# Scaling half of the gate one-hots on ScalarE instead of VectorE

## The chip, the cores and the metric

The kernel runs on one core of a Trainium2 chip. The metric is the device time of one execution in microseconds (us). Below, PE is TensorE, DVE is VectorE, ACT is ScalarE, POOL is GpSimd and SP is the engine that issues most of the transfers.

## The reference, cut to what matters

One encoder block over 512 tokens of width 1024: RMSNorm, a projection, a pooling mixer and forgetting attention, an output projection, and then PEER, a retrieval over 16384 experts. Only PEER is touched by the change:

```
top_s, top_pos = lax.top_k(cand_s, PEER_TOPK)            # 8 heads, 16 picks each, of 128 x 128 experts
gates = jax.nn.softmax(top_s, axis=-1)
a = gelu(einsum('thkd,td->thk', expert_u[idx], xb))
y = einsum('thk,thkd->td', gates * a, expert_v[idx])     # added to x
```

Everything is float32.

## The kernel before, in words

For the first 128 tokens (`FIRST`) the picked expert rows are gathered by indirect transfers and handled on DVE: one `dot` for each of the 128 picks (L1293) and one `add_row` for each (L1423). For the other 384 tokens (`DT`) the kernel works densely: it computes u . x for all 16384 experts in 128 chunks of 128 experts ("ups"), makes a dense gate matrix, multiplies the two and runs 128 chunks of a down product. Every matmul operand is split into a high and a low part (`three`, L746), so that an up chunk is 8 x 3 matmuls of 384 columns. The split of the weights is made by ACT (high part, `hi_to`, L514) and by POOL or DVE (low part).

The gate matrix of one token t is a 128 x 128 matrix: the sum over its 128 picks of gate * onehot(first index) * onehot(second index). That is one matmul of two one-hot matrices, contracted over the picks, one of them scaled by the gates. It is made in the gate stage, which lies under 48 of the up chunks (`UPS_GATE`). Tokens go in groups of four (`GROUP`), 96 groups (`GROUPS`) in all, two for each up chunk (`CHUNK_GROUPS`). `slotT` holds both indices turned so that picks lie on partitions; the turned gates stay in a PSUM bank (`GATE_BANK`).

For group g, with `oh` in two buffers (g % 2):

- DVE, L1403 to L1417: waits until PE has used group g - 2 (`oh_used`), compares (L1408, both one-hots of four tokens in one instruction), does one `dot` in eight of nine groups, waits for its own comparison (`fence`), and multiplies the first one-hot by the gates (L1415), which signals `oh_ready`.
- PE, L996 to L1006: inside an up chunk, ahead of its third and its seventh block of three matmuls (k = 2 and k = 6), waits for `oh_ready` and for a free PSUM bank (`gp_used`), and does the four matmuls of a group, which signal `oh_used`.
- ACT, L703 to L719: for each up chunk first copies both groups from PSUM to `gbuf` (L709, after `oh_used`), then does `up` (L677): the Gelu of the chunk (L683), the high split of the chunk four further on (L514), and each second time a store; then a store of a piece of the gates.

Ahead of the stage ACT copies the two turned index tiles (L698) and the counting row (L700), and does the `up` of the last chunk before the stage (L701). PE turns the gates (`turn(2)`, shown as L976) ahead of the last block of that chunk, and signals `tr_ready`. Each engine works through its instructions in this written order. The end of the up chunks is followed by `residual` (L1017) and by the quads of the down product (L1030), whose first operands come back from DRAM by SP (L386).

Of the kernel before, what the change touches and what calls it, by code (L numbers as in the profile page):

```python
# [8 lines left out]
ALU = mybir.AluOpType  # L9
ACT = mybir.ActivationFunctionType  # L10
AX = mybir.AxisListType

P = 128
# [26 lines left out]
RAW, SPLIT = 3, 4  # L40
# [3 lines left out]
DT = T - FIRST  # L44
# [3 lines left out]
GROUP = 4  # L48
GROUPS = DT // GROUP
# [13 lines left out]
UP_GATE = UP_SOFT + UPS_SOFT  # L63
UP_REST = UP_GATE + UPS_GATE
CHUNK_GROUPS = GROUPS // UPS_GATE
# [17 lines left out]
def program(nc, xvT, wst, consts, w_pool, keysT, uT, u, v, out):  # L83
# [6 lines left out]
    with ctx:  # L90
        def sb(name, shape, dt=F32, where=ctx, side=None):
            return where.enter_context(nc.sbuf_tensor(name, shape, dt, side=side))

        def sem(name):
            return ctx.enter_context(nc.semaphore(name))
# [65 lines left out]
        gates = ExitStack()  # L161
        oh = sb("oh", [P, 2, 2, GROUP, P], where=gates)
        sel = sb("sel", [P, 3, TB, PH, TOPK], where=gates)
        slotT = sb("slotT", [P, 2, DT], where=gates)
        junk = sb("junk", [P, D], BF16, gates)
        gates.close()
        gt.insert(0, sb("gt0", [P, SENT, QUAD * HALF], where=ups))
# [30 lines left out]
        bank = low + [wide[:, 0:T], wide[:, T:2 * T]]  # L198
# [4 lines left out]
        GATE_BANK, IOTA_BANK = 4, 5  # L203
# [34 lines left out]
        gd_ready, ge_ready, sel_ready = sem("gd_ready"), sem("ge_ready"), sem("sel_ready")  # L238
        tr_ready, tr_saved = sem("tr_ready"), sem("tr_saved")
        oh_ready, oh_used, gp_used = sem("oh_ready"), sem("oh_used"), sem("gp_used")  # L240
        gp_stored = [sem("gp_stored0"), sem("gp_stored1")]
        a_out = [sem("a_out0"), sem("a_out1")]
        picks_ready, rows_t_ready = sem("picks_ready"), sem("rows_t_ready")
# [86 lines left out]
        def a_of(j):  # L330

            return act_a[:, (j // 2) % 2, j % 2, :]

        def done_up(j):

            return j - UP_EARLY + NQ + 1
# [163 lines left out]
        def _(act):  # L500
            split = 0

            def hi_to(last):

                nonlocal split
                while split <= min(last, END_W - 1):
                    n, split = split, split + 1
                    if n in POOL_HI:
                        continue
                    act.wait_ge(*landed(n))  # L510
                    if n >= SPLIT:
                        act.wait_ge(w_used, n - SPLIT + 1)
                    part = slice(T, D) if n < 2 else slice(0, D)
                    act.activation(wh[:, n % SPLIT, part], raw_of(n)[:, part], ACT.Copy).then_inc(w_hi, 1)  # L514
# [162 lines left out]
            def up(j):  # L677

                n = UP_W + j - UP_EARLY
                if j % 2 == 0:  # L680
                    act.wait_ge(a_out[(j // 2) % 2], 16 * (j // 4))
                act.wait_ge(w_used, n + 1)
                act.activation(a_of(j), bank[n % 2][:, 0:DT], ACT.Gelu).then_inc(out_done, 1)  # L683
                hi_to(n + SPLIT)
                if j % 2:
                    act.wait_ge(out_done, done_up(j))
                    act.dma_start(a_dram[j // 2], act_a[:, (j // 2) % 2, :, :]).then_inc(a_out[(j // 2) % 2], 16)
# [11 lines left out]
            act.wait_ge(tr_saved, 2)  # L699
            act.activation(bank[IOTA_BANK][:, 0:P], iota, ACT.Copy).then_inc(tr_saved, 1)  # L700
            up(UP_GATE - 1)  # L701

            for j in range(UP_GATE, UP_REST):  # L703
                for g in range(CHUNK_GROUPS * (j - UP_GATE), CHUNK_GROUPS * (j - UP_GATE + 1)):
                    half, at = g // HALF_GROUPS, GROUP * (g % HALF_GROUPS)
                    if at == 0 and half >= 2:
                        act.wait_ge(gp_stored[half % 2], 16 * PIECES * (half // 2))
                    act.wait_ge(oh_used, g + 1)
                    act.activation(gbuf[:, half % 2, :, at:at + GROUP],  # L709
                                   bank[GP + g % 2][:, :].rearrange("j (t i) -> j i t", t=GROUP), ACT.Copy)\  # L710
                       .then_inc(gp_used, 1)
                up(j)
                full, piece = divmod(CHUNK_GROUPS * (j - UP_GATE + 1) // (HALF_GROUPS // PIECES), PIECES)
                if 1 <= full <= SENT:
                    half, rows = full - 1, slice(piece * NCH // PIECES, (piece + 1) * NCH // PIECES)
                    if piece == 0:
                        act.wait_ge(gp_used, FREE_BANKS + HALF_GROUPS * full)
                    act.dma_start(g_dram[half, :, rows, :], gbuf[:, half % 2, rows, :])\
                       .then_inc(gp_stored[half % 2], 16)  # L719
# [25 lines left out]
        def _(pe):  # L745
# [194 lines left out]
            for k in range(NQ):  # L940
# [7 lines left out]
                if k == 3:  # L948
                    pe.wait_ge(identr_ready, 1)
                    for kk in range(KD):  # L950
                        at = slice(kk * P, (kk + 1) * P)
# [6 lines left out]
            def up(n, static, between=None):  # L958

                pe.wait_ge(w_lo, n + 1)  # L960
                pe.wait_ge(out_done, n - (QUERY_W + 1))
                project(bank[static % 2][:, 0:DT], static % SPLIT, hh, hl, between, at=slice(FIRST, T))
# [31 lines left out]
            with pe.Fori(0, UPS_GATE // SPLIT) as it:  # L994
                for i in range(SPLIT):
                    def frames(k):  # L996
                        if k % 4 != 2:
                            return
                        of = CHUNK_GROUPS * i + k // 4
                        group = it * (CHUNK_GROUPS * SPLIT) + of  # L1000
                        pe.wait_ge(oh_ready, group + 1)
                        pe.wait_ge(gp_used, group + 1)
                        for t in range(GROUP):
                            last = pe.matmul(bank[GP + of % 2][:, t * P:(t + 1) * P], oh[:, of % 2, 1, t, :],  # L1004
                                             oh[:, of % 2, 0, t, :], start=True, stop=True)
                        last.then_inc(oh_used, 1)  # L1006

                    static = UP_W + UP_GATE - UP_EARLY + i
                    up(it * SPLIT + static, static, frames)
# [3 lines left out]
            def residual(b, done):  # L1013

                for half in range(2):
                    for kk in range(4):
                        last = pe.matmul(bank[done + half][:, kk * P:(kk + 1) * P], x[:, 4 * half + kk, b * P:(b + 1) * P],  # L1017
                                         ident, start=(kk == 0), stop=(b == 0 and kk == 3), is_transpose=True)
                return last

            pe.wait_ge(gp_used, FREE_BANKS + GROUPS)
            pe.wait_ge(oh_ready, GROUPS)
            residual(2, 2)
            residual(3, 4)
            pe.wait_ge(dots_done, PICKS)
# [32 lines left out]
        def _(dve):  # L1058
# [8 lines left out]
            def step(instruction):  # L1067

                nonlocal count
                count += 1  # L1070
                instruction.then_inc(dve_done, 1)

            def fence():

                dve.wait_ge(dve_done, count)
# [35 lines left out]
            for what, i in in_turn:  # L1111
# [45 lines left out]
                if what == "norm":  # L1157
                    n, c = i, i // 2
                    dst, g = (qn, QG) if i % 2 == 0 else (kn, KG)
# [64 lines left out]
                elif what == "mean":  # L1224
                    g, z = i, len(QK_W) + i
# [5 lines left out]
                    src, s = 0, 1  # L1231
                    while s < w:
# [4 lines left out]
                        src, s = dst, 2 * s  # L1237
# [15 lines left out]
                elif what == "score":  # L1253
# [16 lines left out]
                    for b in blocks:  # L1270
                        at, size = P if b == 1 else 0, (b + 1) * P
# [21 lines left out]
            def dot(j):  # L1293

                if j == 0:
                    dve.wait_ge(rows_t_ready, 1)
                dve.wait_ge(row_in[j % ROWS], 16 * (j // ROWS + 1))
                if j:
                    dve.wait_ge(dots_done, j)
                dve.scalar_tensor_tensor(junk[:, :], picked[:, j % ROWS, :], 1.0, wide[:, :], ALU.mult, ALU.mult,  # L1300
                                         accum_out=pick_a[:, j:j + 1]).then_inc(dots_done, 1)
# [101 lines left out]
            for g in range(GROUPS):  # L1403
                s, at = g % 2, slice(GROUP * g, GROUP * g + GROUP)
                if g >= 2:
                    dve.wait_ge(oh_used, g - 1)
                both = [P, 2, GROUP, P]
                step(dve.tensor_tensor(oh[:, s], bank[IOTA_BANK][:, 0:P].unsqueeze(1).unsqueeze(1).broadcast_to(both),  # L1408
                                       slotT[:, 0:2, at].unsqueeze(3).broadcast_to(both), ALU.is_equal))
                if g % 9 != 8 and g < GROUPS - 1:  # L1410
                    dot(DOTS_GATE + g - g // 9)
                fence()
                if g == 0:
                    dve.wait_ge(tr_ready, 3)
                dve.tensor_tensor(oh[:, s, 0], oh[:, s, 0],  # L1415
                                  bank[GATE_BANK][:, at].unsqueeze(2).broadcast_to([P, GROUP, P]), ALU.mult)\
                   .then_inc(oh_ready, 1)  # L1417
# [130 lines left out]
```

## Time and profile before

| | |
|---|---|
| time, median of 3 runs | 1440.97 us (1440.34 to 1442.09) |
| profiled execution | 1441.41 us |
| its span | 1439.4 us |
| PE busy | 1431.6 us (99%) |
| DVE busy | 1133.4 us (79%) |
| ACT busy | 574.4 us (40%) |
| POOL busy | 979.8 us (68%) |
| gate stage | about 596 to 883 us of the span |

A busy share is the time in which an engine executes instructions, as a share of the span; PE can be near 100% in stages in which it waits for nobody and in which only its own work counts. The order in which engines wait for one another stands in the waits and in the timeline.

### The profile page before, as it was taken

How to read it: one execution, taken by the hardware profiler on the slowest of the kernel's cores; microseconds unless marked ns; L12 is line 12 of the kernel's file. 1: busy time of each engine (PE TensorE's matmuls, PEld its weight loads, DVE VectorE, ACT ScalarE, POOL GpSimd, SP SyncE). 2: the span in 40 equal slices, each digit the busy share in tenths (PEclk: the TensorE clock that was granted, in tenths of full speed). 3: DMA queues.
4: the chain of work that ended last, by engine and by line, in shares of the span. 5: the costliest groups of instructions: out<-in, count | busy, mean ns of one | idle time of the engine just before them, and what ended most of it. 6: DMA issues, size and time to landing. Idle time of an engine off the chain costs nothing.

```text
span 1439.4 us, 20447 instructions
## 1 busy us (share of the span) xinstructions
PE 1431.6 (99%) x7551; PEld 1277.2 (89%) x7551; DVE 1133.4 (79%) x1876; ACT 574.4 (40%) x799; POOL 979.8 (68%) x533
## 2 busy tenths in 40 slices
PE   9999999999999999999999999999999999999998
PEld 7766798899999999999999999888888888888887
DVE  6678551769999999699999995498777777777775
ACT  5775453333333333444444444333333333333332
POOL 3421544346888788866766675599887888878883
PEclk9999999999999999999999999999999999999999
DMA  6221332235778888989999986998888888888883
GB/s 227 103 89 45 103 113 100 89 100 184 251 262 268 273 272 273 348 281 364 355 360 355 372 296 230 371 383 340 346 346 346 327 326 345 344 341 328 331 302 117
DMA packets 122293, 381.57 MB, mean 265 GB/s; under 512 B 11768, under 2 KB 28280, under 8 KB 122240
## 3 DMA queue, kind: packets, MB, share of 16 engines
q1 hardware_dynamic: 70384, 202.69, 39.5%
q0 software_dynamic: 36864, 134.23, 25.3%
q10 hardware_dynamic: 14992, 44.06, 7.8%
q8 instruction: 18, 0.29, 0.1%
q14 instruction: 35, 0.29, 0.1%
HBM read 336.89 MB, written 44.06 MB: 265 GB/s over the span
## 4 chain that ended last, share of the span: by engine, by line
PE 95%; DVE 2%; DMA 1%; ACT 1%; issue 0%; SPq 0%; DVEq 0%
PE bank L748 28%; PE bank L749 28%; PE bank L750 28%; PE bank L1004 6%; PE bank L936 1%; DMA wf<-a_dram 1%; PE bank L884 1%; PE bank L907 0%; PE wide L896 0%; DVE pad L1235 0%; PE bank L815 0%; PE wide L815 0%; PE bank L826 0%; PE bank L822 0%; PE wide L822 0%
## 5 line engine op out<-in xcount | busy, mean ns | idle before, releaser
L484 POOL TENSOR_TENSOR wl<-raw,wh 128x1024 fp32r<-128x1024 f32 x208 | 507.7, 2442 | 277.7 <-ACT wh L514 275.1
L748 PE MATMUL bank<-hh,wh 128*128 128x384 f32 (+1 forms) x1184 | 416.2, 352 | 0.2 <-DVE hl L1251 0.2
L749 PE MATMUL bank<-hl,wh 128*128 128x384 f32 (+1 forms) x1184 | 406.4, 343 | 0.0
L750 PE MATMUL bank<-hh,wl 128*128 128x384 f32 (+1 forms) x1184 | 406.4, 343 | 0.0
L748 PE MATMUL bank<-wh,Wh 128*128 128x512 f32 x768 | 299.0, 389 | 0.7 <-DVE Wl L1458 0.7
L750 PE MATMUL bank<-wh,Wl 128*128 128x512 f32 x768 | 298.8, 389 | 0.0
L749 PE MATMUL bank<-wl,Wh 128*128 128x512 f32 x768 | 298.8, 389 | 0.0
L514 ACT ACTIVATE wh<-raw 128x1024 fp32r<-128x1024 f32 (+1 forms) x217 | 227.8, 1050 | 141.4 <-PE bank L750 136.4
L748 PEld LDWEIGHTS bank<-hh,wh 128*128 128x128 f32 x1184 | 222.8, 188 | 7.9 <-DVE hl L1251 0.6
L749 PEld LDWEIGHTS bank<-hl,wh 128*128 128x128 f32 x1184 | 222.8, 188 | 7.1 <-issue 0.2
L750 PEld LDWEIGHTS bank<-hh,wl 128*128 128x128 f32 x1184 | 222.3, 188 | 7.6
L494 POOL DMA_INDIRECT picked<-v_dram,picks x128 | 200.5, 1567 | 24.9 <-issue 21.7
L748 PEld LDWEIGHTS bank<-wh,Wh 128*128 128x128 f32 x768 | 144.1, 188 | 30.9 <-issue 1.2
L750 PEld LDWEIGHTS bank<-wh,Wl 128*128 128x128 f32 x768 | 144.1, 188 | 30.1
L749 PEld LDWEIGHTS bank<-wl,Wh 128*128 128x128 f32 x768 | 144.1, 188 | 29.8
L1300 DVE SCALAR_TENSOR_TENSOR junk<-picked,wide 128x1024 bf16<-128x1024 f32 x128 | 155.1, 1212 | 12.3 <-DMA picked<-u_dram,picks 10.1
L1432 DVE SCALAR_TENSOR_TENSOR wide<-picked,pick_a,wide 128x1024 f32<-128x1024 f32 x128 | 163.8, 1280 | 0.5
L484 POOL TENSOR_TENSOR wl<-xraw,wh 128x1024 fp32r<-128x1024 f32 x54 | 131.1, 2428 | 43.5 <-ACT wh L514 42.9
L514 ACT ACTIVATE wh<-xraw 128x1024 fp32r<-128x1024 f32 x72 | 76.4, 1061 | 199.1 <-PE bank L750 181.9
L683 ACT ACTIVATE act_a<-bank 128x384 f32<-128x384 f32 x124 | 61.0, 492 | 224.8 <-PE bank L750 210.9
L494 POOL DMA_INDIRECT picked<-u_dram,picks x128 | 130.1, 1016 | 29.3 <-issue 14.1
L1408 DVE TENSOR_TENSOR oh<-bank,slotT 128x1024 f32<-128x1024 f32 x96 | 117.5, 1224 | 12.1 <-PE bank L1004 8.6
(200 smaller groups left out, 1628.6 us busy)
## 6 DMA issues: line engine op xcount, KB each, us to landing
raw<-uT_dram SPq DMA_DIRECT2D x128, 512.0 KB
xraw<-v_dram SPq DMA_DIRECT2D x72, 512.0 KB, 8.5
raw<-v_dram SPq DMA_DIRECT2D x56, 512.0 KB, 9.1
a_dram<-act_a ACTq DMA_DIRECT2D x64, 384.0 KB
wf<-a_dram SPq DMA_DIRECT2D x32, 768.0 KB, 6.8
raw<-wst_dram SPq DMA_DIRECT2D x40, 512.0 KB
gates_dram<-gbuf ACTq DMA_DIRECT2D x32, 512.0 KB
gt<-gates_dram SPq DMA_DIRECT2D x32, 512.0 KB, 4.0
```

Source lines behind the costliest of these rows:

```text
L484: pool.tensor_tensor(wl[:, n % SPLIT, :], raw_of(n), wh[:, n % SPLIT, :].bitcast(F32), ALU.subtract).then_inc(w_lo, 1)
L494: pool.indirect_dma_start(out=picked[:, j % ROWS, :], out_offset=None, in_=u if j < PICKS else v_rows, in_offset=bass.IndirectOffsetOnAxis ...
L514: act.activation(wh[:, n % SPLIT, part], raw_of(n)[:, part], ACT.Copy).then_inc(w_hi, 1)
L683: act.activation(a_of(j), bank[n % 2][:, 0:DT], ACT.Gelu).then_inc(out_done, 1)
L748: pe.matmul(dst, ah, bh, start=start, stop=False)
L749: pe.matmul(dst, ah, bl, start=False, stop=False)
L750: return pe.matmul(dst, al, bh, start=False, stop=stop)
L884: last = pe.matmul(bank[S_BANK + o][:, at:at + (b + 1) * P], qn[rows, c, b * P:(b + 1) * P], kn[rows, c, 0:(b + 1) * P], start=True, stop= ...
L1004: last = pe.matmul(bank[GP + of % 2][:, t * P:(t + 1) * P], oh[:, of % 2, 1, t, :], oh[:, of % 2, 0, t, :], start=True, stop=True)
L1300: dve.scalar_tensor_tensor(junk[:, :], picked[:, j % ROWS, :], 1.0, wide[:, :], ALU.mult, ALU.mult, accum_out=pick_a[:, j:j + 1]).then_inc ...
L1408: step(dve.tensor_tensor(oh[:, s], bank[IOTA_BANK][:, 0:P].unsqueeze(1).unsqueeze(1).broadcast_to(both), slotT[:, 0:2, at].unsqueeze(3).br ...
L1432: dve.scalar_tensor_tensor(wide[:, :], picked[:, j % ROWS, :], pick_a[:, i:i + 1], wide[:, :], ALU.mult, ALU.add).then_inc(first_added, 1)
```

## The change

Every odd group of one-hots is no longer multiplied on DVE. DVE compares and signals `oh_equal`; ACT, at the head of its work for each up chunk, waits for that, and scales the first one-hot of the chunk's odd group in place with four activations, one for each token, the gates of the token being a per-partition scale pointer; each signals `oh_scaled`. ACT reads the gates from SBUF, from a third tile in `slotT`, which it copies from `GATE_BANK` once, ahead of the stage and after the `up` at L701. The multiplication of group 0 on DVE now waits for that copy. PE waits for `oh_scaled` at odd groups and for `oh_ready` at even ones.

```
-        slotT = sb("slotT", [P, 2, DT], where=gates)
+        slotT = sb("slotT", [P, 3, DT], where=gates)
...
 @block.scalar
             up(UP_GATE - 1)
+            act.wait_ge(tr_ready, 3)
+            act.activation(slotT[:, 2, 0:DT], bank[GATE_BANK][:, 0:DT], ACT.Copy).then_inc(tr_saved, 1)
+            act.wait_ge(tr_saved, 4)
 
             for j in range(UP_GATE, UP_REST):
+                odd = CHUNK_GROUPS * (j - UP_GATE) + 1
+                act.wait_ge(oh_equal, odd // 2 + 1)
+                for t in range(GROUP):
+                    act.activation(oh[:, odd % 2, 0, t, :], oh[:, odd % 2, 0, t, :], ACT.Copy,
+                                   scale=slotT[:, 2, GROUP * odd + t:GROUP * odd + t + 1]).then_inc(oh_scaled, 1)
                 for g in range(CHUNK_GROUPS * (j - UP_GATE), CHUNK_GROUPS * (j - UP_GATE + 1)):
...
 @block.tensor
-                        pe.wait_ge(oh_ready, group + 1)
+                        if of % 2:
+                            pe.wait_ge(oh_scaled, it * (GROUP * SPLIT) + GROUP * (i + 1))
+                        else:
+                            pe.wait_ge(oh_ready, it * SPLIT + (i + 1))
                         pe.wait_ge(gp_used, group + 1)
...
-            pe.wait_ge(oh_ready, GROUPS)
+            pe.wait_ge(oh_ready, GROUPS // 2)
+            pe.wait_ge(oh_scaled, GROUP * (GROUPS // 2))
...
 @block.vector
-                step(dve.tensor_tensor(oh[:, s], ... ALU.is_equal))
+                equal = dve.tensor_tensor(oh[:, s], ... ALU.is_equal)
+                if g % 2:
+                    equal.then_inc(oh_equal, 1)
+                else:
+                    step(equal)
                 if g % 9 != 8 and g < GROUPS - 1:
                     dot(DOTS_GATE + g - g // 9)
+                if g % 2:
+                    continue
                 fence()
                 if g == 0:
-                    dve.wait_ge(tr_ready, 3)
+                    dve.wait_ge(tr_saved, 4)
                 dve.tensor_tensor(oh[:, s, 0], oh[:, s, 0],
                                   bank[GATE_BANK][:, at].unsqueeze(2).broadcast_to([P, GROUP, P]), ALU.mult)\
                    .then_inc(oh_ready, 1)
```

## Rows read from the trace of the kernel before

**Rows 1.** Waits of PE, whole span: who waited for whom, us, times, longest.
```profile
PE bank L781 <- DVE pm L1077: 1.5, 1, 1.5
...
PE bank L748 <- DVE Wl L1458: 0.7, 1, 0.7
```
**Rows 2.** Groups of DVE, 596 to 884 us: busy, mean ns, idle before.
```profile
L1408 DVE TENSOR_TENSOR oh<-bank,slotT 128x1024 f32<-128x1024 f32 x96 | 117.5, 1224 | 12.1 <-PE bank L1004 8.6 <-ACT bank L700 2.4
...
L1415 DVE TENSOR_TENSOR oh<-oh,bank 128x512 f32<-128x512 f32 x96 | 65.6, 683 | 0.4
```
**Rows 3.** Timeline, middle of the gate stage: start, us, instruction.
```profile
700.15 1.05 ACT L514 ACTIVATE wh<-raw 128x1024 fp32r<-128x1024 f32 x1
700.54 1.05 PE L1004 MATMUL bank<-oh 128*128 128x128 f32 x8
701.63 1.23 DVE L1408 TENSOR_TENSOR oh<-bank,slotT 128x1024 f32<-128x1024 f32 x1 [1.02 <-PE bank L1004]
...
703.34 1.03 PEld L1004 LDWEIGHTS bank<-oh 128*128 128x128 f32 x8
703.91 0.68 DVE L1415 TENSOR_TENSOR oh<-oh,bank 128x512 f32<-128x512 f32 x1
704.60 0.60 ACT L709 ACTIVATE gbuf<-bank 128x512 f32<-128x512 f32 x1 [2.37 <-PE bank L1004]
705.64 0.49 ACT L683 ACTIVATE act_a<-bank 128x384 f32<-128x384 f32 x1 [0.44 <-issue]
706.32 1.03 PEld L1004 LDWEIGHTS bank<-oh 128*128 128x128 f32 x8
```
**Rows 4.** Timeline, start of the gate stage.
```profile
594.81 0.86 ACT L698 ACTIVATE slotT<-bank 128x384 f32<-128x384 f32 x2
597.54 0.49 PE L976 MATMUL bank<-cst,sel 128*128 128x128 f32 x3
598.29 0.68 DVE L1415 TENSOR_TENSOR oh<-oh,bank 128x512 f32<-128x512 f32 x1
598.89 1.22 DVE L1408 TENSOR_TENSOR oh<-bank,slotT 128x1024 f32<-128x1024 f32 x1
598.97 1.05 ACT L514 ACTIVATE wh<-raw 128x1024 fp32r<-128x1024 f32 x1
599.28 1.03 PEld L1004 LDWEIGHTS bank<-oh 128*128 128x128 f32 x8
...
601.76 1.22 DVE L1408 TENSOR_TENSOR oh<-bank,slotT 128x1024 f32<-128x1024 f32 x1
```
**Rows 5.** The chain that ended last, first gate matmuls: start, us, what.
```profile
599.61 0.89 PE bank L1004 x8
602.58 0.89 PE bank L1004 x8
```
**Rows 6.** Timeline, ups after the gate stage, the second left out.
```profile
884.04 0.49 ACT L683 ACTIVATE act_a<-bank 128x384 f32<-128x384 f32 x1 [0.44 <-PE bank L750]
...
892.37 0.49 ACT L683 ACTIVATE act_a<-bank 128x384 f32<-128x384 f32 x1 [2.66 <-PE bank L750]
```
**Rows 7.** Groups of ACT by form, whole span: busy, mean ns, idle before.
```profile
L603 ACT ACTIVATE pr<-pr,edges 128x128 f32<-128x128 f32 x8 | 3.2, 395 | 2.1 <-DVE edges L1273 2.0
L618 ACT ACTIVATE pT<-wide 128x128 f32<-128x128 f32 x8 | 2.2, 279 | 0.0
L596 ACT ACTIVATE hh<-bank,xv 128x512 fp32r<-128x512 f32 x4 | 2.8, 688 | 4.4 <-PE bank L871 4.4
L625 ACT ACTIVATE hh<-bank 128x512 fp32r<-128x512 f32 x4 | 2.4, 599 | 11.4 <-PE bank L907 11.4
```
**Rows 8.** The chain that ended last, around the down product's start.
```profile
914.14 11.10 DMA wf<-a_dram
...
929.55 0.49 PE bank L748
```
**Rows 9.** Busy time and granted clock by stretch: PE, PEld, DVE, ACT, POOL, PEclk, DMA, GB/s.
```profile
700.00:740.00 40.00, 40.00 (x273) 40.00 (x272) 37.77 (x51) 17.61 (x27) 27.78 (x19) 1.00 0.98 364
...
925.00:930.00 5.00, 4.26 (x19) 3.22 (x18) 4.67 (x4) 1.06 (x1) 1.99 (x1) 1.00 1.04 412
```

More of the change, by code:

```diff
@@ L240, in program @@
         oh_ready, oh_used, gp_used = sem("oh_ready"), sem("oh_used"), sem("gp_used")
+        oh_equal, oh_scaled = sem("oh_equal"), sem("oh_scaled")
         gp_stored = [sem("gp_stored0"), sem("gp_stored1")]
@@ L1407, in _ @@
                 both = [P, 2, GROUP, P]
-                step(dve.tensor_tensor(oh[:, s], bank[IOTA_BANK][:, 0:P].unsqueeze(1).unsqueeze(1).broadcast_to(both),
-                                       slotT[:, 0:2, at].unsqueeze(3).broadcast_to(both), ALU.is_equal))
+                equal = dve.tensor_tensor(oh[:, s], bank[IOTA_BANK][:, 0:P].unsqueeze(1).unsqueeze(1).broadcast_to(both),
+                                          slotT[:, 0:2, at].unsqueeze(3).broadcast_to(both), ALU.is_equal)
+                if g % 2:
+                    equal.then_inc(oh_equal, 1)
+                else:
+                    step(equal)
                 if g % 9 != 8 and g < GROUPS - 1:
                     dot(DOTS_GATE + g - g // 9)
+                if g % 2:
+                    continue
                 fence()
                 if g == 0:
-                    dve.wait_ge(tr_ready, 3)
+                    dve.wait_ge(tr_saved, 4)
                 dve.tensor_tensor(oh[:, s, 0], oh[:, s, 0],
```

## The prediction

> **What bounds the kernel now.** I read the busy shares first: PE is busy for 1431.6 of 1439.4 us, so it can be waiting for almost nothing. The waits of PE say where: the longest is 1.5 us at the very start, the only one behind the gate stage is 0.7 us at the start of the down product, and none is a wait for a one-hot [rows 1]. Then I asked whether the gate stage is nevertheless paced by DVE, since DVE is busy there for 37.8 of 40 us [rows 9]. The timeline answers. In the middle of the stage PE loads the weights of a group at 703.34 and of the next at 706.32, that is every 2.97 us, and DVE's multiplication for a later group had ended at 704.59, 1.7 us before the second of these [rows 3]. At the start of the stage DVE turned out a group each 2.87 us (the comparisons start at 598.89 and 601.76 [rows 4]) while PE already took 2.97 us (599.61 and 602.58 [rows 5]). So DVE is the faster of the two, PE keeps its own pace from the first group on, and DVE ends up waiting for it: 8.6 us before L1408 [rows 2]. The stage is PE's.
>
> **What the change takes away.** 48 multiplications on DVE at 683 ns, 32.8 us of DVE [rows 2]. In the stage they lie beside PE's matmuls, and the DVE wait grows by as much. Gain on the path: 0. Bounds: not below 0, and at most what PE's pace holds above its own work. An up chunk without gates takes (892.37 - 884.04) / 2 = 4.17 us [rows 6] (with two groups, 2 x 2.97 = 5.95 us), so one group's eight gate passes cost (5.95 - 4.17) / 2 = 0.89 us, which is just what they span in the chain [rows 5]. Nothing is left over by this, and the one or two hundredths that the rounding may hide in each group would be 1 to 2 us over 96 groups. I take 0 and keep 2 us as the other end.
>
> **What it adds on ACT, in the steady state.** Four activations of 128x128 from SBUF to SBUF with a pointer as scale, per chunk. This form isn't in the trace. The nearest rows: a plain copy of 128x128 from PSUM took 279 ns; an Exp of 128x128 with a pointer as bias, in place, 395 ns; and at 128x512 a scale pointer makes 688 ns of 599, 89 ns more [rows 7]. So 279 at least, 279 + 89 = 368 by the pair, 395 at most; I take 385, since the Exp row is nearest in operands. Two activations in a row took 0.86 us [rows 4], and one of their size, 128x384, takes 0.49 (L683, [rows 3]), so that successive ones overlap by about 0.11 us. Four then take 4 x 0.385 - 3 x 0.11 = 1.2 us (1.6 without any overlap).
>
> Does that fit? ACT is in order, so I lay it beside PE's clock. Gelu and high split of the chunk before end at 700.15 + 1.05 = 701.20 [rows 3], 0.66 us after the even group's matmuls began. The odd comparison is long done then: it starts when PE has used the odd group before, at about 698.7 (2.97 us before 701.63), and ends at 699.9. So the scalings run from 701.2 to 702.4, and PE wants the odd group when it loads its weights at 703.34: 0.9 us to spare (0.5 with 1.6 us). What is queued behind them on ACT is the copy of the even group (0.60 us), now from about 702.4 instead of 701.6 to 703.0; PE wants its bank only two groups on, after 706. The copy of the odd group starts at 704.60 as before, with 0.44 us of idle ahead of the Gelu at 705.64 [rows 3]. In the sum ACT goes from 17.6 to about 26 of 40 us [rows 9]. Cost on the path: 0. The cover is 0.9 us per chunk; from where four scalings take more than 2.14 us (703.34 - 701.20), each tenth more costs PE 48 x 0.1 = 4.8 us, because ACT's start in a chunk hangs on PE's end of the chunk before and nothing catches up.
>
> By the Trainium skill, ScalarE: Activation LUTs, What ACT_TABLE_LOAD costs, an ACTIVATE costs a fixed time plus 0.833 ns per element, 93 ns more for each pointer, and overlaps the next by 93 ns. By that page, as an estimate, four would take 4 x 386 - 3 x 93 = 1265 ns, and the slack would be 0.87 us; the table of rules on the same page gives multiplications to VectorE, and indeed the trace has DVE do four tokens in 683 ns. Both speak against the change only if ACT's time is on the path.
>
> **What it adds at the start of the stage.** This is where I see a cost. The multiplication of group 0 waited for PE's turned gates: `turn(2)` ended at 598.03 and the multiplication ran from 598.29 to 598.97, in time for PE's load at 599.28 [rows 4], with 0.3 us to spare. Now it waits for ACT's copy of them, and that copy stands behind the `up` of the last chunk, whose high split ran from 598.97 to 600.02. With the overlap of 0.11 us the copy starts at 599.92 and ends at 600.41 (0.49 us). With 0.04 us for the semaphore (gate matmuls end at 701.59, DVE starts at 701.63 [rows 3]) DVE multiplies from 600.45 to 601.13, and PE loads at about 601.2 instead of 599.28: 1.9 us in which PE has nothing it may do, as it is in order. Lower bound 1.7 (copy dispatched sooner), upper 2.2.
>
> Behind this stall: DVE's comparison of group 1 moves from 598.89 to 601.05 and ends at 602.3; ACT, idle by then, scales until 603.5; PE wants it at 601.2 + 2.97 = 604.2. 0.6 us to spare, the tightest place of the stage. Then comparison 2 follows the dot of group 1 at 603.4, its multiplication ends at 606.3, and PE wants it at 607.1. After that DVE needs 2.87 + 2.27 = 5.1 us per chunk (the even group's 2.87, and 0.6 less for the odd) against 5.95, and gains its lead back. The dot of group 1 is 2.1 us later, so POOL's next gather and the low split behind it are too; that split is of a chunk that PE reads two chunks on. Nothing is added.
>
> **Does the 1.9 us come back later?** Only where PE waits anyway for something that does not hang on PE. After the ups, PE's one wait is 0.7 us at 929.55, for `Wl`, at the end of a transfer of 11.10 us that was issued at 914.14, behind PE's own residual matmuls [rows 1, 8]. As the issue hangs on PE it moves with it. If the transfers (busy at 1.04 in that stretch, [rows 9]) ended sooner for having had 1.9 us more, at most 0.7 us would return. I take 0.
>
> **The sum.** 0 (DVE) + 0 (steady ACT) + 1.9 (start) + 0 (later) = +1.9 us. The profiled execution took 1441.41 us, 2.0 more than its span, so one of after should take 1443.3, with a span of 1441.3. The median of the runs is 0.44 us lower than the profiled one: 1440.97 + 1.9 = 1442.9 us.
>
> **Rivals.**
>
> *The scalings come too late in every chunk* (the slower side). Place: PE's wait for `oh_scaled` at k = 6. For it: ACT is in order, the form of activation is unmeasured here, and the slack is under 1 us. It decides from a pitch of 0.535 us per activation (2.14 / 4). If each cost what the 128x512 form with a pointer does, 0.69 us without overlap, four would take 2.75 us, 0.6 over: 48 x 0.6 + 1.9 = +31 us, 1472. Against it: every 128x128 row is under 0.40. A mild form, in which some chunks miss by a tenth or two because ACT's split waits for a transfer, gives +2 to +6 us.
>
> *The start costs nothing, or comes back.* If ACT's copy were done by 598.6 (ahead of the split), the time stays at 1441.0. For it: little, since the order is written out. With the 0.7 us of the down product back, 1442.2.
>
> *PE gains from a lighter stage* (faster). If part of PE's 2.97 us is friction with DVE's accesses, the most I found is 2 us: 1442.9 - 2 = 1440.9, no change. For a measurable gain PE would have to have waited for DVE, which rows 1 and rows 4 against rows 5 exclude. By this the change does what it says, frees DVE, and nobody was waiting for DVE.
>
> *The clock falls after the stall.* The granted clock was 1.00, the 2.4 GHz level, in the stretch with PE's 0.74 us wait [rows 9]; nothing shows it after 1.9 us. If PE ran at 1.2 GHz for one chunk behind the stall, that is 5.95 us more: 1448.9. The Trainium skill, TensorE: Matmul & The Clock Gate, The HAM clock gate, says that the clock follows how busy PE has lately been; by that such a fall is possible after any pause, and no row here decides it.
>
> **How the numbers follow.** A measurement here can tell about 0.2% (2.9 us) from no change. Forecast (+1 to +2.8): 0.68. Nothing or back, and friction gained: 0.14. Scalings late, in the mild form 0.08, in the strong one 0.03. Clock: 0.05. Something in DVE's favour that I don't see: 0.02. From the forecast's case a tenth could still measure above 2.9 us. So faster 0.04, same 0.76, slower 0.20. The range holds the forecast, the case of nothing with its 2 us of friction, and the mild slower forms: 1440.3 to 1446.0.
>
> **What would show it.** Right: PE's waits get one new line, L1004 on DVE's L1415, about 1.9 us, once, near 601; PE's gate matmuls keep their 2.97 us from there to the end; L1415 has 48 instructions, the new ACT line 192 at 0.37 to 0.40 us; DVE's idle time before L1408 grows from 12 to some 45 us; the wait for `Wl` stays near 0.7. Wrong: a wait of PE on the new ACT line; a pitch other than 2.97; no wait near 601; or a granted clock under 1.00 there.

## The result and the profile after

| | before | after |
|---|---|---|
| time, median of 20 runs | 1440.41 us (1440.06 to 1442.09) | 1442.89 us (1442.32 to 1443.98) |
| profiled execution, its span | 1441.41, 1439.4 us | 1442.33, 1440.4 us |
| PE, DVE, ACT busy | 1431.6, 1133.4, 574.4 us | 1431.9, 1097.7, 628.0 us |

The ratio after to before is 1.0016 (95% interval 1.0010 to 1.0022): slower by about 2.3 us, or 2.5 by the medians. The interval excludes 1, so this small loss is clear of the noise, though it is less than the 0.2% that the prediction took as the least that a measurement can tell.

DVE's busy time fell by 36 us, of which the 48 multiplications are 32.8; the rest is within what the unchanged kernel varies by (1126.9 us in its second profile, e8 below). ACT took on 54 us, PE kept its own. The waits of PE after (who waited for whom: us in total, times, longest) have one new line, the first. Two of before are gone: the one of 0.7 us at the start of the down product, and one of 0.4 us in the first microseconds of the span (`mh`):

```profile
PE bank L1016 <- DVE oh L1434: 1.7, 1, 1.7
PE bank L790 <- DVE pm L1090: 1.5, 1, 1.5
PE bank L779 <- DVE sq_low L1183: 1.3, 1, 1.3
PE bank L757 <- DVE hl L1264: 0.2, 1, 0.2
```

The start of the gate stage after, in the timeline, answers to [rows 4]. L704 is the new copy of the gates, L1434 DVE's multiplication, L711 ACT's scaling, L1016 the gate matmuls, L1421 the comparison:

```profile
598.92 1.05 ACT L515 ACTIVATE wh<-raw 128x1024 fp32r<-128x1024 f32 x1
599.87 0.48 ACT L704 ACTIVATE slotT<-bank 128x384 f32<-128x384 f32 x1
600.46 0.69 DVE L1434 TENSOR_TENSOR oh<-oh,bank 128x512 f32<-128x512 f32 x1 [2.12 <-ACT slotT L704]
601.06 1.22 DVE L1421 TENSOR_TENSOR oh<-bank,slotT 128x1024 f32<-128x1024 f32 x1
601.28 0.97 PEld L1016 LDWEIGHTS bank<-oh 128*128 128x128 f32 x8 [2.04 <-issue]
601.28 1.15 PE L1016 MATMUL bank<-oh 128*128 128x128 f32 x8 [1.72 <-DVE oh L1434]
602.37 1.29 ACT L711 ACTIVATE oh<-oh,slotT 128x128 f32<-128x128 f32 x4 [2.02 <-DVE oh L1421]
604.21 1.03 PEld L1016 LDWEIGHTS bank<-oh 128*128 128x128 f32 x8
```

Copy behind the split, multiplication behind the copy, PE behind the multiplication: PE loads at 601.28 where it loaded at 599.28. The middle of the stage after answers to [rows 3]:

```profile
702.11 1.05 ACT L515 ACTIVATE wh<-raw 128x1024 fp32r<-128x1024 f32 x1
702.33 1.03 PEld L1016 LDWEIGHTS bank<-oh 128*128 128x128 f32 x8
703.06 1.27 ACT L711 ACTIVATE oh<-oh,slotT 128x128 f32<-128x128 f32 x4
703.59 1.22 DVE L1421 TENSOR_TENSOR oh<-bank,slotT 128x1024 f32<-128x1024 f32 x1 [1.75 <-PE bank L1016]
704.24 0.58 ACT L718 ACTIVATE gbuf<-bank 128x512 f32<-128x512 f32 x1
705.31 1.03 PEld L1016 LDWEIGHTS bank<-oh 128*128 128x128 f32 x8
```

The four scalings end at 704.33, 0.98 us before PE loads the odd group; PE's loads are 2.98 us apart, as before. DVE now sits idle before each second comparison. The groups of the stage after, answering to [rows 2]: 48 multiplications less, and the idle time before the comparisons up from 12.1 to 41.5 us; the new activation has a mean of 393 ns:

```profile
L1421 DVE TENSOR_TENSOR oh<-bank,slotT 128x1024 f32<-128x1024 f32 x96 | 117.6, 1225 | 41.5 <-PE bank L1016 37.4 <-ACT bank L701 3.6
...
L711 ACT ACTIVATE oh<-oh,slotT 128x128 f32<-128x128 f32 x192 | 61.4, 393 | 3.6 <-DVE oh L1421 2.0 <-issue 0.9
...
L1434 DVE TENSOR_TENSOR oh<-oh,bank 128x512 f32<-128x512 f32 x48 | 32.8, 684 | 2.3 <-ACT slotT L704 2.1
```

### The profile page after: what moved, and what is told of

It is laid out like the page before. It is cut to its first block, busy times and chain, and to the rows that moved or that the text cites. A ratio compares the mean times of both kernels' runs of the same rounds, so it can differ in the third digit from the quotient of the medians.

```text
span 1440.4 us, 20593 instructions
## 1 busy us (share of the span) xinstructions
PE 1431.9 (99%) x7551; PEld 1277.6 (89%) x7551; DVE 1097.7 (76%) x1828; ACT 628.0 (44%) x992; POOL 975.4 (68%) x533
## 4 chain that ended last, share of the span: by engine, by line
PE 97%; DVE 2%; ACT 1%; issue 0%; DVEq 0%
PE bank L757 28%; PE bank L759 28%; PE bank L758 28%; PE bank L1016 6%; PE bank L945 1%; PE bank L893 1%; PE bank L916 0%; PE wide L905 0%; DVE pad L1248 0%; PE bank L790 0%; PE bank L824 0%; PE wide L824 0%; PE wide L831 0%; PE bank L831 0%; PE bank L835 0%
## 5 line engine op out<-in xcount | busy, mean ns | idle before, releaser
L485 POOL TENSOR_TENSOR wl<-raw,wh 128x1024 fp32r<-128x1024 f32 x208 | 507.6, 2442 | 280.0 <-ACT wh L515 277.4
L495 POOL DMA_INDIRECT picked<-v_dram,picks x128 | 196.1, 1532 | 24.8 <-issue 20.9
L1421 DVE TENSOR_TENSOR oh<-bank,slotT 128x1024 f32<-128x1024 f32 x96 | 117.6, 1225 | 41.5 <-PE bank L1016 37.4
```

What stands on the lines that cost most here:

```text
L485: pool.tensor_tensor(wl[:, n % SPLIT, :], raw_of(n), wh[:, n % SPLIT, :].bitcast(F32), ALU.subtract).then_inc(w_lo, 1)
L495: pool.indirect_dma_start(out=picked[:, j % ROWS, :], out_offset=None, in_=u if j < PICKS else v_rows, in_offset=bass.IndirectOffsetOnAxis ...
L1421: equal = dve.tensor_tensor(oh[:, s], bank[IOTA_BANK][:, 0:P].unsqueeze(1).unsqueeze(1).broadcast_to(both), slotT[:, 0:2, at].unsqueeze(3) ...
```

## The experiments

Medians below are of 11 runs each where nothing else is said (e4 5, e5 and e6 4, e9 7). The kernel before, beside them on the same chips, had 1440.61 us (beside e1 to e4), 1440.69 (e5 to e8) and 1440.84 (e9). One of its 27 executions behind the first of these took 4919 us; the median does not feel it.

### e2_stall: only the wait, nothing moved to ACT

```
 (the kernel before)
+            act.wait_ge(tr_ready, 3)              # behind up(UP_GATE - 1)
+            act.activation(slotT[:, 2, 0:DT], bank[GATE_BANK][:, 0:DT], ACT.Copy).then_inc(tr_saved, 1)
+            act.wait_ge(tr_saved, 4)
...
                 if g == 0:
-                    dve.wait_ge(tr_ready, 3)
+                    dve.wait_ge(tr_saved, 4)
```

> The kernel before, to which only the copy of the turned gates to SBUF on ACT is added behind the last up before the stage, and for which DVE's multiplication of group 0 waits. All multiplications stay on DVE. My theory: the same stall as in the changed kernel, 1.7 to 1.9 us at the first gate matmul, and the same time as the changed kernel, 1442.4 to 1443. After the stall DVE has no shorter odd groups to recover with, but its 2.87 us per group is still under PE's 2.97, so nothing is added. Rival A (part of the loss is the ACT work): 1440.9 to 1442. Rival B (DVE, without relief, stays late behind the stall and PE waits again): over 1443.5.

Measured: 1442.33 us (1441.96 to 1444.45). The timeline of its stage start:

```profile
599.74 0.48 ACT L703 ACTIVATE slotT<-bank 128x384 f32<-128x384 f32 x1
600.33 0.69 DVE L1418 TENSOR_TENSOR oh<-oh,bank 128x512 f32<-128x512 f32 x1 [2.12 <-ACT slotT L703]
601.07 1.16 PE L1007 MATMUL bank<-oh 128*128 128x128 f32 x8 [1.63 <-DVE oh L1418]
```

The same stall, and by the medians 1.7 to 2.0 us over the kernel before (1440.61 beside it, 1440.32 for e8 below). The median lies just under the range given for it, 0.6 us under the changed kernel's. In the profiled executions the two kernels end alike: both spans are 1440.4 us, and the last matmul starts at 1436.35 us here and at 1436.34 in the changed kernel.

### e7_early and e1_direct: the offload without the wait

e7 puts the copy ahead of the last up; e1 leaves the copy behind it and lets group 0 do without it:

```
 (e7, from the changed kernel)                       (e1, from the changed kernel)
+            act.wait_ge(tr_ready, 3)               -            act.wait_ge(tr_ready, 3)
+            act.activation(slotT[:, 2, ...         +            act.wait_ge(oh_ready, 1)
+            act.wait_ge(tr_saved, 4)               ...
             up(UP_GATE - 1)                        -                if g == 0:
-            act.wait_ge(tr_ready, 3)               -                    dve.wait_ge(tr_saved, 4)
-            act.activation(slotT[:, 2, ...         +                if g in (0, 2):
-            act.wait_ge(tr_saved, 4)               +                    dve.wait_ge(*((tr_saved, 4) if g else (tr_ready, 3)))
```

All three kernels, these two and the changed one, still read the gates of the even groups from `GATE_BANK` on DVE, not from ACT's copy. The wait only keeps ACT's read of the bank and DVE's apart; in e7 and in the changed kernel ACT reads first, in e1 DVE does.

> The changed kernel with ACT's copy of the turned gates put ahead of the last up instead of behind it. ACT then copies from about 598.1 to 598.6 us, and DVE multiplies group 0 from 598.65 to 599.35. My theory: PE's wait at the first gate matmul shrinks from 1.7 to about 0.1 us, and the time is 1440.5 to 1441.5, as e1_direct (1441.38). Rival (the position of the copy does not matter, as something else delays the multiplication): 1442.5 or more.

> The changed kernel, except that DVE's multiplication of group 0 again waits only for PE's turned gates; ACT copies them after that multiplication, and DVE's next multiplication (group 2) waits for the copy. My theory (the whole loss is the one stall at the first gate matmul): PE's wait at the gate matmul is gone, PE loads group 0 at 599.3 us as before, the gate matmuls keep their pitch of 2.97 us, and the time is that of before, 1440.4, within 0.5 us. Rival A (ACT's added work also costs PE something in steady state, or somewhere later): at least 0.5 us of the loss of 2.5 remains, 1440.9 or more. Rival B (DVE's relief is worth something that the stall hid): below 1440.0.

Measured: e7 1440.42 us (1440.29 to 1441.42), e1 1441.38 us (1440.92 to 1442.15). In e7 the copy comes early enough, and the matmul line of PE has no wait at a gate matmul; its weight loads sit idle for 0.19 us ahead of the first group:

```profile
598.11 0.49 ACT L703 ACTIVATE slotT<-bank 128x384 f32<-128x384 f32 x1 [2.08 <-PE bank L985]
598.71 0.69 DVE L1434 TENSOR_TENSOR oh<-oh,bank 128x512 f32<-128x512 f32 x1 [0.28 <-ACT slotT L703]
599.53 0.97 PEld L1016 LDWEIGHTS bank<-oh 128*128 128x128 f32 x8 [0.19 <-issue]
599.54 1.15 PE L1016 MATMUL bank<-oh 128*128 128x128 f32 x8
```

So the offload with the wait mended costs nothing and brings nothing, within 0.1% (the ratio to before is 1.0000, 0.9991 to 1.0009). e1 missed: 0.8 us remained, which is rival A's sign, though its interval (0.9996 to 1.0014) still holds 1. Its trace does not put them into the gate stage. Its first and last gate matmuls start at 599.50 and 881.97, 282.47 us apart; before it was 599.45 and 881.91, 282.46. Nor are they ahead of the last matmul, which starts at 1434.41 us in e1 and at 1434.31 in e8, the second profile of before. The difference is behind all matmuls, in SP's last wait, which is for the output to be stored (first e1, then e7):

```profile
SPq L90 <- DMA out_dram<-gbuf: 3.2, 1, 3.2
```

```profile
SPq L90 <- DMA out_dram<-gbuf: 2.3, 1, 2.3
```

All four kernels built with e1's order (e1, e3, e4, e6) show 3.2 us here, and the seven others 2.3, one profile each. So it goes with the kernel rather than with the single run, and e1's loss is rival A's "somewhere later". How an order of waits some 830 us earlier lengthens the last store is open. In e1 the transfers have all but ended before the wait does: they move 221 GB/s from 1437 to 1438 us and 12 from 1438 to 1439, and the span ends at 1439.4.

### e8_before_again: how much the ends vary

The kernel before, unchanged.

> The kernel before, unchanged, as a look at how much the parts of the span that hang on transfers vary: the first profile had 0.7 us of PE waiting at the start of the down product, and 3.6 us from ACT's last copy to the end of the span; e1_direct had none and 4.6 us. If these vary from run to run, this profile shows another pair (0 and 3.6, by the median of 1440.6 us), and e1_direct's 0.8 us above before is the tail. If it shows 0.7 and 3.6 again, the tail isn't the reason. Time: the same as before, within 0.3 us.

Measured: 1440.32 us (1440.01 to 1441.08); its profiled execution took 1440.44 with a span of 1438.4. Its waits of PE:

```profile
PE bank L781 <- DVE pm L1077: 1.5, 1, 1.5
PE bank L770 <- DVE sq_low L1170: 1.3, 1, 1.3
PE bank L748 <- DVE hl L1251: 0.2, 1, 0.2
```

The 0.7 us wait at the start of the down product is not there: it comes and goes, and the profile from which I predicted had caught one of its occurrences (that execution took 1441.41 us, 1.0 above the median of 20). From the last gate matmul to the first matmul of the down product it is 46.86 us in the first profile of before, 45.96 here, 45.97 after and 46.26 in e7, so up to 0.9 us of a single execution hangs on this place. The end does not vary in the same way: the last wait for the output is 2.3 us in both profiles of before, so the tail of e1 is no such coming and going. Against this profile the last matmul of the changed kernel starts 2.03 us later (1434.31 and 1436.34): the stall alone.

### e3_act1 and e4_act12: how much ACT may take

```
 (e1_direct)
+        dump = sb("dump", [P, 768], BF16, gates)
...
                 act.wait_ge(oh_equal, odd // 2 + 1)
+                for i in range(0, 768, 768):      # e4: range(0, 768, 64)
+                    act.activation(dump[:, i:i + 768], flat[:, i:i + 768], ACT.Copy)      # e4: 64
```

> e1_direct with one more activation per up chunk on ACT, ahead of the four scalings: a copy of 128x768 to a scratch tile, about 0.82 us, 0.73 with the overlap. In the trace of the changed kernel the scalings end at 704.33 and PE loads the odd group at 705.31, 0.98 us later. My theory (ACT's work is free up to that slack): same time as e1_direct, within 0.5 us, no wait of PE for the scalings. Rival (ACT's work costs in proportion, by its share or by contention): 48 x 0.73 = up to 35 us more.

> e1_direct with twelve activations of 128x64 to a scratch tile per up chunk ahead of the four scalings; each 0.24 us, pitch 0.15, together about 1.75 us. My theory (each chunk loses what ACT's block exceeds the slack of 0.98 by): 48 x 0.77 = 37 us more than e1_direct, 1477 (between 1470 and 1485), in one wait per chunk of PE for the scalings, about 0.77 us. Rival (PE or ACT catches up, as ACT runs ahead in other places): under 10 us more.

Measured: e3 1441.91 us (1441.59 to 1442.61), e4 1482.62 us (1482.38 to 1483.97). e3 adds about 0.73 us to every chunk, 35 us in all, and the time rises by 0.5, just beyond what I allowed. The matmul line of PE has no wait for the scalings in it, but its stage is 0.4 us longer (599.22 to 882.12). About 0.25 of these lie at the first odd group, the tightest place of the stage: the scalings end at 602.22, and the weight loads sit idle until 602.34. The rest is spread in steps of a few hundredths, which nothing here explains.

```profile
600.96 1.26 ACT L715 ACTIVATE oh<-oh,slotT 128x128 f32<-128x128 f32 x4
...
602.34 0.74 PEld L1020 LDWEIGHTS bank<-oh 128*128 128x128 f32 x6 [0.30 <-issue]
```

In e4 the block overruns the slack, and each of the 48 chunks pays. The timeline of one:

```profile
703.38 1.86 ACT L713 ACTIVATE dump<-sel 128x64 bf16<-128x64 f32 x12
705.13 1.27 ACT L715 ACTIVATE oh<-oh,slotT 128x128 f32<-128x128 f32 x4
706.53 0.97 PEld L1020 LDWEIGHTS bank<-oh 128*128 128x128 f32 x8 [0.88 <-issue]
706.53 1.15 PE L1020 MATMUL bank<-oh 128*128 128x128 f32 x8 [0.56 <-ACT oh L715]
```

and the two lines of its waits between 590 and 930 us that bear on it:

```profile
PEld bank L1020 <- issue: 43.3, 48, 1.8
...
PE bank L1020 <- ACT oh L715: 28.2, 48, 1.5
```

e4 is 41.2 us slower than e1, near the 37 expected. This agrees with the 0.98 us of slack in the profile of after: added work of 0.73 us per chunk is under it and nearly free, 1.75 us is over it and costs 0.86 per chunk. Between the two no run was made.

### e5_half_before and e6_half_direct: where DVE's relief is worth something

Two of the four tokens' gate matmuls are left out in both, so that PE's group is shorter.

```
-                        for t in range(GROUP):
+                        for t in range(GROUP // 2):
```

> The kernel before with PE doing only the matmuls of the first two of each group's four tokens (the other two tokens' gate matrices are left out; everything that DVE and ACT do stays). It shortens PE's group from 2.97 to about 2.53 us, and DVE's 2.87 us (1.73 in each ninth, without a dot) stays. My theory: now DVE paces the stage, its mean over nine groups is (8 x 2.87 + 1.73) / 9 = 2.74 us, so the stage takes 96 x 2.74 = 263 us instead of 285, PE waits for DVE's multiplication, some 20 us in all, and the time is 1440.5 - 22 = 1418. Rival (DVE was pacing the stage already, or something else than PE): the time stays within 5 us of 1440.5.

> The same omission of half of the gate matmuls, made in e1_direct, where ACT scales the odd groups. My theory: DVE needs 5.1 us per chunk and PE 5.06, so PE's own pace holds, but for small waits: 48 x 0.89 = 43 us less than e1_direct, 1398 to 1402. The relief of DVE is then worth 16 to 20 us against e5_half_before, while at full matmuls it is worth nothing. The slack of the scalings does not shrink below zero: PE reaches the odd group 0.45 us sooner after the chunk's start, and 0.98 - 0.45 = 0.5 us remain. Rival A (ACT comes too late for the shorter chunk): 1410 or more, with PE waiting for the scalings. Rival B (transfers, at 0.97 of their time busy in the stage, become the bound): over 1405 with PE waiting for weights.

Measured: e5 1420.85 us (1419.90 to 1422.99), e6 1405.88 us (1403.95 to 1409.66). e5 is 20 us below before, where I expected 22. Now DVE paces the kernel before: PE's weight loads wait for its multiplications 53 times, 21.2 us in all. In e5 PE's loads follow DVE's multiplications every 2.87 us, which is DVE's own pace in [rows 4]:

```profile
703.12 0.68 DVE L1415 TENSOR_TENSOR oh<-oh,bank 128x512 f32<-128x512 f32 x1
703.86 0.52 PEld L1004 LDWEIGHTS bank<-oh 128*128 128x128 f32 x4 [0.37 <-DVE oh L1415]
...
706.73 0.52 PEld L1004 LDWEIGHTS bank<-oh 128*128 128x128 f32 x4 [0.39 <-DVE oh L1415]
```

From the first gate load to the last there are 263.6 us in e5 (263 expected) and 246.0 in e6. By the medians the same offload that is worth 0 with all matmuls is worth 15 us here, just under the 16 to 20 expected. e6 missed its 1398 to 1402 by about 4 us: of its 95 steps from one gate group to the next some 80 are PE's own 2.53 us, and the others together are about 5.6 us longer. Neither of its rivals is the reason as I put them: PE waited for no weights, and hardly for the scalings. What shows is in DVE: its dots wait for gathered rows, and ACT's scalings for DVE's comparisons (waits in e6, 590 to 880 us):

```profile
DVE junk L1313 <- DMA picked<-u_dram,picks: 11.6, 11, 3.6
...
ACT oh L711 <- DVE oh L1421: 8.5, 10, 1.4
```

### e9_parts: a version that is faster than both

The half-work runs say what has to shrink: PE's gate matmuls, and that then the offload counts.

```
 (e7_early; the split of the gates and the bfloat16 copies of the indices are left out here)
-        oh = sb("oh", [P, 2, 2, GROUP, P], where=gates)
+        oh = sb("oh", [P, 2, 4, GROUP, P], BF16, gates)      # two one-hots, the first by the high and by the low part
+        part = sb("part", [P, 2, DT], BF16, gates)           # high and low part of the gates
...
 @block.scalar
-                    act.activation(oh[:, odd % 2, 0, t, :], oh[:, odd % 2, 0, t, :], ACT.Copy,
-                                   scale=slotT[:, 2, GROUP * odd + t:GROUP * odd + t + 1]).then_inc(oh_scaled, 1)
+                    for a in (2, 3):
+                        act.activation(oh[:, odd % 2, a, t, :], oh[:, odd % 2, 0, t, :], ACT.Copy,
+                                       scale=slotT[:, a - 2, GROUP * odd + t:GROUP * odd + t + 1]).then_inc(oh_scaled, 1)
...
 @block.tensor
-                            last = pe.matmul(bank[GP + of % 2][:, t * P:(t + 1) * P], oh[:, of % 2, 1, t, :],
-                                             oh[:, of % 2, 0, t, :], start=True, stop=True)
+                            for a in (2, 3):
+                                last = pe.matmul(bank[GP + of % 2][:, t * P:(t + 1) * P], oh[:, of % 2, 1, t, :],
+                                                 oh[:, of % 2, a, t, :], start=a == 2, stop=a == 3)
...
 @block.vector
-                dve.tensor_tensor(oh[:, s, 0], oh[:, s, 0],
-                                  bank[GATE_BANK][:, at].unsqueeze(2).broadcast_to([P, GROUP, P]), ALU.mult)\
+                dve.tensor_tensor(oh[:, s, 2:4], oh[:, s, 0:1].broadcast_to(both),
+                                  part[:, :, at].unsqueeze(3).broadcast_to(both), ALU.mult).then_inc(oh_ready, 1)
```

> A version that is meant to be faster, built on e7_early: the one-hots become bfloat16 (exact for 0 and 1), the gates are split into a high and a low bfloat16 part, and PE does two bfloat16 matmuls per token, accumulated, instead of the float32 one, which the trace shows as two matmul instructions of two passes each. DVE makes both scaled one-hots of an even group in one multiplication of 128x1024, ACT those of an odd group in eight activations. The gates keep about 16 bits. By the half-work experiments PE's group shrinks from 2.97 to about 2.53 us. My theory: then ACT sets the pace. Its eight scalings take 2.45 us and start 0.7 us after PE's load of the even group; PE wants the odd group 2.53 us after that load, so it is late by about 0.6 us per chunk: of 43 us gained 31 are lost again, and the time is 1440.4 - 12 = 1428 (1420 to 1435), with PE waiting for the scalings. Rival A (DVE sets the pace: 1.14 + 1.13 + 1.14 + 2.27 = 5.7 us per chunk): about the same time, but PE's waits on DVE's line. Rival B (PE's bfloat16 matmuls of 128 columns are no faster in sum, as their weight loads of 0.19 us set the pace): 1440 or more.

Measured: 1437.60 us (1436.25 to 1438.14), ratio to before 0.9973 (0.9962 to 0.9984). It is the fastest here of the kernels that do all of the work, but the gain is 3 us where I expected 12. The waits of PE:

```profile
PE bank L1022 <- ACT oh L716: 18.7, 47, 0.9
PE bank L1022 <- DVE oh L1444: 4.3, 4, 3.2
```

ACT's eight scalings pace it, as expected, once per chunk. I had left out the start of the stage: splitting the gates makes PE wait 3.2 us, and the first gate matmul starts at 602.68, 3.1 us later than in e7. The stage itself is shorter by 5.9 us, not by 12 (from the first gate matmul to the last 277.4 us, in e7 283.4). The pace that I had reckoned with holds for most of it: the median chunk takes 5.72 us, where I had about 5.7. But ten of the 47 steps from chunk to chunk take 5.87 to 6.77 us, 4.7 us more in all, so that the mean is (880.1 - 602.7) / 47.5 = 5.84. In the longest of these ACT itself waits for DVE's comparison, as DVE's dots wait for gathered rows again (waits in e9, 590 to 890 us):

```profile
DVE junk L1319 <- DMA picked<-u_dram,picks: 9.1, 7, 1.9
...
ACT oh L716 <- DVE oh L1427: 6.5, 5, 3.2
```

Half of the 6.5 us is the one wait at the start of the stage. DVE has little margin here: it is idle for only 7 us before its comparisons in the stage.

## Why the prediction was right

- **PE bounds the stage, DVE does not.** Right: 33 us less DVE work in the stage left PE's pitch at 2.98 us, and e7 has the time of before. The argument that DVE ran at 2.87 us at the stage's start was the decisive one: e5 shows just that pace once PE is made shorter.
- **ACT's block fits.** Right in kind and size: 1.27 us for four, where I took 1.2, and 0.98 us to spare, where I took 0.9. e3 and e4 lie on either side of the edge. The pointer activation took 393 ns, so the Exp row in [rows 7] was the right neighbour. The estimate of 1265 ns, worked out from the figures of the Trainium skill, ScalarE: Activation LUTs, What ACT_TABLE_LOAD costs, agrees with the trace too, which has 1.27 us for the four.
- **The start of the stage.** Right, step by step: multiplication at 600.46 (600.45 predicted), PE's load at 601.28 (601.2), the tightest place behind it 0.55 us (602.37 + 1.29 to 604.21; 0.6 predicted). e2 has the stall without the offload, e7 the offload without the stall; each behaves as its part. The size was 2.03 us on PE's last matmul, where I took 1.9.
- **Nothing comes back.** Right against e8, though the profile of after seemed to say otherwise: its span is only 1.0 us over that of the first profile of before. The other 1.0 is in that first profile: 0.9 at the start of the down product, where the 0.7 us wait of [rows 1] lies, which e8 does not have, and the rest ahead of the gate stage. I had expected that wait to stay ("the wait for `Wl` stays near 0.7"), and so forecast a profiled execution of 1443.3 us with a span of 1441.3; they were 1442.33 and 1440.4. The wait belongs to single executions.
- **The sum.** 1442.9 predicted, 1442.89 measured. That the two agree to a hundredth is luck. The rise over the median of 20 runs is 2.5 us, not 1.9: the base I started from, a median of three, was 0.6 us high. Of the 2.5, the stall is 2.0; the other 0.5 appear between the profiled execution of after (1442.33) and its median (1442.89), so no trace that I have shows them. It may be the same kind of coming and going as at the start of the down product, but that is open.
- **The rivals.** No scaling came late, the granted clock stayed at 1.00, the 2.4 GHz level, through the stall and behind it (596 to 620 us), and DVE's relief was worth nothing. Still open is why the last wait for the output is 3.2 us in e1 and the three kernels built on it and 2.3 in all others; no experiment was made on it.

## What to carry to other kernels

An engine that is 95% busy is not the bound as long as its own cycle, read where it is running free, is shorter than that of the engine it feeds; moving work off it is then worth nothing, and every new wait that comes with the move is paid in full. Look for such a wait at the first turn of the loop, where a value is taken from a new place by an engine whose order puts it behind unrelated work. When work is added to an in-order engine, measure its slack to the next deadline: under it the work here was all but free, over it each turn paid the excess. The first turn can have less slack than the others, as in e3.

## What the runs showed of the hardware that I had not expected

- A wait of PE costs more than PE's idle time says. In e4 PE's matmul queue idled 28.2 us for the scalings, but its weight loads idled 43.3, and the time rose by 41.2. In the stalled kernel 1.72 and 2.04, and the last matmul moved by 2.03. Each of e4's waits has 0.59 us of idle time. To this come 0.16 us by which matmuls otherwise overlap (in the middle of the stage before one of 0.33 us starts at 702.99 and the next at 703.17), and 0.10 us by which the group behind the wait is itself longer (1.15 us instead of 1.05). That makes 0.85, and 41.2 / 48 is 0.86. Without a wait the loads run about 0.17 us ahead of the matmuls (load at 703.34, matmuls from 703.51), and in e4 both start at 706.53, so that in these float32 runs the line of the weight loads comes near the price. That is no rule for all: in e9, in bfloat16, the loads idled 46.1 us in the 96 groups, of which 0.16 us ahead of nearly every even group. Its matmuls start on their usual beat there, so these gaps cost nothing:

```profile
700.80 0.45 PEld L1022 LDWEIGHTS bank<-oh 128*128 128x128 bf16 x8 [0.16 <-issue]
700.80 0.62 PE L1022 MATMUL bank<-oh 128*128 128x128 bf16 x8
```

- The weight loads of 128x128 in e9 took 98 ns in bfloat16 against 191 ns in float32, so that the eight loads of a group span 0.45 us against 1.03; its eight matmuls span 0.62 us against 1.05.
- In e9 DVE's conversion of 128x384 from float32 to bfloat16 took 1.56 us, from 599.72 to 601.28, while POOL's subtraction ran from 598.68 to 601.05; a DVE subtraction of the same size just ahead took 0.56. It looks as if the conversion waited for POOL to finish. That was seen once and not tested.
